# Second and fourth feed-forward of a fused FP32 transformer kernel: the norm's token factor moved from the input rows to the gate and up results

## The reference, cut to what matters

```python
def rms_norm(x, g):
    y = xf * lax.rsqrt(jnp.mean(xf * xf, axis=-1, keepdims=True) + EPS)
    return y * g
def modulate(h, shift, scale):
    return h * (1.0 + scale[:, None, :]) + shift[:, None, :]
def swiglu(h, w_in, w_out):
    g, u = jnp.split(h @ w_in, 2, axis=-1)          # 1024 -> 2 x 2816
    return (jax.nn.silu(g) * u) @ w_out             # 2816 -> 1024
h = modulate(rms_norm(x, norm_g), sh, sc)
x = x + 0.5 * (1.0 + gate)[:, None, :] * swiglu(h, w_in, w_out)
```

## Time and profile before

| | |
|---|---|
| median of 3 runs | 1314.43 us |
| profiled execution, whole | 1312.69 us |
| its span, first to last instruction | 1310.9 us |
| TensorE matmul busy | 1258.1 us (96%) |
| VectorE busy | 1068.6 us (82%) |
| ScalarE busy | 633.6 us (48%) |
| chain that ended last | PE 88%, DVE 7%, ACT 2% |
| granted TensorE clock, mean | 0.994 of full |

### The profile page before, as it was taken

One profiled execution on the slowest core, in us unless ns is written; L12 is line 12 of the kernel. 1 busy time (PEld: TensorE's weight loads), 2 busy tenths in 40 slices (PEclk: granted clock), 3 DMA queues, 4 the chain that ended last, 5 costly groups with the idle time before them and its releaser, 6 DMA issues.

```text
span 1310.9 us, 26643 instructions
## 1 busy us (share of the span) xinstructions
PE 1258.1 (96%) x10570; PEld 1227.8 (94%) x10570; DVE 1068.6 (82%) x1668; ACT 633.6 (48%) x994; POOL 187.2 (14%) x203
## 2 busy tenths in 40 slices
PE   1999999999999999999999999999999999999996
PEld 1999999899999889999999999999999989999996
DVE  6998988898787777988878778999977588895674
ACT  2534334443434556554346653343455675455453
POOL 5598800000000000000001000000000014530000
PEclk8999999999999999999999999999999999999999
DMA  9998887399888359988863379887655698555561
GB/s 356 394 329 314 295 316 270 131 319 336 304 311 286 129 193 358 331 303 306 309 207 112 113 245 331 302 304 262 217 179 184 114 186 179 169 163 178 175 194 50
DMA packets 110924, 319.73 MB, mean 244 GB/s; under 512 B 24096, under 2 KB 35808, under 8 KB 110560
## 3 DMA queue, kind: packets, MB, share of 16 engines
q1 hardware_dynamic: 110816, 318.23, 73.0%
HBM read 313.18 MB, written 5.01 MB: 243 GB/s over the span
## 4 chain that ended last, share of the span: by engine, by line
PE 88%; DVE 7%; ACT 2%; issue 1%; DMA 1%; SPq 1%; ACTq 0%; DVEq 0%
PE tiles L375 18%; PE tiles L377 18%; PE tiles L376 18%; PE acc L375 8%; PE acc L376 8%; PE acc L377 8%; PE nrm L551 1%; DVE w_lo L367 1%; PE tiles L577 1%; DVE arena L1474 1%; PE tiles L579 1%; PE tiles L594 1%; DMA arena<-in_gstream 1%; ACT w_hi L363 1%; DVE arena L1429 1%
## 5 line engine op out<-in xcount | busy, mean ns | idle before, releaser
L363 ACT CAST w_hi<-land 128x1024 fp32r<-128x1024 f32 x391 | 408.4, 1047 | 452.1 <-PE tiles L377 282.4
L367 DVE TENSOR_TENSOR w_lo<-land,w_hi 128x1024 fp32r<-128x1024 f32 x391 | 484.0, 1245 | 145.9 <-ACT w_hi L363 144.6
L375 PE MATMUL tiles<-x_hi,w_hi 128*128 128x256 f32 x1384 | 393.8, 285 | 0.8 <-DVE arena L1874 0.5
L376 PE MATMUL tiles<-x_lo,w_hi 128*128 128x256 f32 x1384 | 391.9, 283 | 0.0
L377 PE MATMUL tiles<-x_hi,w_lo 128*128 128x256 f32 x1384 | 391.8, 283 | 0.0
L375 PEld LDWEIGHTS tiles<-x_hi,w_hi 128*128 128x128 f32 x1384 | 265.7, 192 | 3.0 <-issue 1.0
L376 PEld LDWEIGHTS tiles<-x_lo,w_hi 128*128 128x128 f32 x1384 | 265.8, 192 | 0.1
L377 PEld LDWEIGHTS tiles<-x_hi,w_lo 128*128 128x128 f32 x1384 | 265.8, 192 | 0.0
L1429 DVE SCALAR_TENSOR_TENSOR arena<-arena 128x1024 f32<-128x1024 f32 x184 | 227.2, 1239 | 12.3 <-ACT arena L1157 9.5
L375 PE MATMUL acc<-h_hi,w_hi 128*128 128x256 f32 x704 | 199.4, 283 | 0.0
L376 PE MATMUL acc<-h_lo,w_hi 128*128 128x256 f32 x704 | 199.3, 283 | 0.0
(11 more groups left out here) (338 smaller groups left out, 1601.1 us busy)
## 6 DMA issues: line engine op xcount, KB each, us to landing
land<-in_stream SPq DMA_DIRECT2D x391, 512.0 KB, 4.5
arena<-in_gstream SPq DMA_DIRECT2D x184, 512.0 KB, 6.4
w_dram<-arena SPq DMA_DIRECT2D x3, 512.0 KB, 6.4
arena<-w_dram SPq DMA_DIRECT2D x6, 256.0 KB, 9.2
arena<-in_c_rows SPq DMA_DIRECT2D x2, 512.0 KB, 5.7
x<-in_x_t SPq DMA_DIRECT2D x1, 1024.0 KB, 9.5
arena<-in_ssm_bn SPq DMA_DIRECT2D x1, 1024.0 KB, 8.6
u_dram<-arena SPq DMA_DIRECT2D x1, 1024.0 KB, 5.3
```

The source lines that it names most:

```text
L363: nc.scalar.copy(w_hi[:, u % RING], land[:, u % LAND]).then_inc(hi_done, 1)
L367: nc.vector.tensor_tensor(w_lo[:, u % RING], land[:, u % LAND], w_hi[:, u % RING].bitcast(F32), ALU.subtract).then_inc(lo_done, 1)
L375: nc.tensor.matmul(outs, lh, rh, start=first, stop=False, **kw)
L376: nc.tensor.matmul(outs, lh, rl, start=False, stop=False, **kw)
```

## The change

Only FFN 1 and FFN 3 (`LATE`) are changed. Their input rows no longer hold the token factor or the shift: ScalarE makes x_hi as x times the feature factor (`late_rows` of ScalarE), VectorE x_lo of the same. To each k row of 256 tokens two more columns are added that hold the shift (`late_shift`), so every gate and up matmul has 258 columns, and column 256 of a result is what the shift contributes to it. Gate and up get a PSUM bank each (`quad`, four banks). For each tile, ScalarE copies the two shift results out (`late_shifts`), VectorE multiplies gate and up by the token factor (`late_scale`, 128 x 512), ScalarE does silu with the shift as bias (`late_silu`), VectorE adds the up shift and multiplies (`late_hidden`), ScalarE makes the high part (`late_hi`), VectorE the low part (`late_lo`). One weight split stands between each two of these on both engines. TensorE's order becomes g0 u0 g1 u1 g2 o0 u2 g3 o1 u3 and so on to g21 o19 u21 o20 o21; the weights are stored in that order.

The squares' sum is taken inside `first_units`, between the products with the high and those with the low input, over four tiles that VectorE has added in pairs. The filler products ahead of both feed-forwards go. On VectorE the coefficients of FFN 1, its shift columns and one weight split move ahead of the pooling updates; at the end of both feed-forwards one weight split moves from before the updates of x to behind them.

```diff
-            sum_squares(2)
-            keep_busy(7)
-            ffn(1, 2)
+            ffn_late(1, 2)
...
+            def pair_sums(e):
+                for k in range(0, KT, 2):
+                    pe.wait_ge(sq_pair, 4 * e + k // 2 + 1)
+                    m = nc.tensor.matmul(late_sum, ones, t_buf[:, k], start=(k == 0), stop=(k == KT - 2))
+                m.then_inc(nrm_done, 1)
+            def ffn_late(f, stage):
+                wait_bank(pe, o0)
+                wait_bank(pe, o0 + 1)
+                pe.wait_ge(shift_cols, 2 * (e + 1))
+                first_units(base, [quad[:, b, 0:T + 2] for b in range(3)], xs_hi, xs_lo, KT * stage,
+                            between=lambda: pair_sums(e))
+                late_unit(3, base + 3, 0)
...
+                            pe.wait_ge(silu_done, i * 4 + (FFN_TILES * f + j - 1))
+                            late_unit(2 * (j % 2), g_unit(f, j), i)
+                            out_unit(f, j - 2, o_unit(f, j - 2), i, 4)
+                            pe.wait_ge(freed["d"], i * 4 + (nd + j - 1))
+                            late_unit(2 * (j % 2) + 1, u_unit(f, j), i)
...  ScalarE
+            def late_rows(stage, n, ready, unit, before=None):
+                nc.scalar.activation(eps_root, con("eps", 1), ACT.Sqrt)
+                for k in range(KT):
+                    ready(k)
+                    nc.scalar.activation(x_hi[:, k], x[:, k], ACT.Identity,
+                                         scale=coef[:, stage, k:k + 1]).then_inc(xh_done, 1)
+                for k in range(KT):
+                    nc.scalar.square(t_buf[:, k], x[:, k]).then_inc(sq_done, 1)
+                split_hi(act, unit)
+                split_hi(act, unit + 1)
+                act.wait_ge(nrm_done, n + 1)
+                nc.scalar.activation(rx_late, late_sum, ACT.Sqrt, bias=con("eps", 1), scale=1.0 / D)
+                nc.scalar.activation(eps_root, con("eps", 1), ACT.Silu)
...
+                            late_shifts(f, j - 2, i, 4)
+                            split_hi(act, o_unit(f, j - 2), i)
+                            late_silu(f, j - 2, i, 4)
+                            split_hi(act, u_unit(f, j), i)
+                            late_hi(f, j - 2, i, 4)
+                            split_hi(act, u_unit(f, j) + 1, i)
...  VectorE
+            norm_coef(2)
+            late_shift(2, 0)
+            split_lo(dve, UNIT["ffn1"] + 1)
             for k in range(KT):
                 wait_tile(dve, TILE["pool"] + k)
                 update(k, tiles[:, k % 2, 0:T], 1, freed["d"])
-            split_lo(dve, UNIT["ffn1"] + 1)
-            norm_coef(2)
             split_lo(dve, UNIT["ffn1"] + 2)
-            root(2)
-            norm_t(2)
+            late_rows(2, 2, 0, UNIT["ffn1"] + 3)
...
+            def late_rows(stage, n, e, unit):
+                (8 x) x_lo = x * factor - x_hi
+                (4 x) t_buf[k] = t_buf[k] + t_buf[k + 1]
+                split_lo(dve, unit)
+                split_lo(dve, unit + 1)
+                dve.wait_ge(rt_done, n + 1)
+                link(V.reciprocal(rx_late, rx_late))
...
+                            late_scale(f, j - 2, i, 4)
+                            (s = 0) split_lo(o(j-2)); late_hidden(f, j - 2, i, 4)
+                            (s = 1) split_lo(u(j)); late_lo(f, j - 2, i, 4)
+                            (s = 2) split_lo(g(j+1))
```

More of the change, by code:

```diff
@@ L589, in first_units @@
                         high(c, k)
+                if between is not None:
+                    between()
                 for c in range(3):
@@ new lines, in late_hi, with ffn_late @@
+            def late_hi(f, j, i, per):
+                nd = OWNER[:TILE[f"ffn{f}"]].count("d")
+                act.wait_ge(freed["d"], i * per + (nd + j + 1))
+                act.wait_ge(used, i * 3 * per + (FFN_BASE[f] + 3 * j))
+                nc.scalar.copy(h_hi[:, j % 2], gate_up[:, j % 2, 1]).then_inc(late_hh, 1)
+            def ffn_late(f):
+                base = FFN_BASE[f]
+                j0 = 2
+                for part, (reps, _) in enumerate(SEGMENTS[f]):
+                    with act.Fori(0, reps) as i:
+                        for m in range(4):
+                            j = j0 + m
+                            late_shifts(f, j - 2, i, 4)
[4 more added lines that the diff above has]
+                            split_hi(act, u_unit(f, j) + 1, i)
+                    j0 += 4 * reps
+                late_shifts(f, FFN_TILES - 2, 0, 0)
+                late_silu(f, FFN_TILES - 2, 0, 0)
+                late_hi(f, FFN_TILES - 2, 0, 0)
+                late_shifts(f, FFN_TILES - 1, 0, 0, 0, 1)
+                split_hi(act, base + 65)
+                late_silu(f, FFN_TILES - 1, 0, 0)
+                split_hi(act, base + 66)
+                late_shifts(f, FFN_TILES - 1, 0, 0, 1, 1)
+                late_hi(f, FFN_TILES - 1, 0, 0)
@@ L1436, in hidden @@
             def hidden(f, j, i, per):
-                base, nd = FFN_BASE[f], OWNER[:TILE[f"ffn{f}"]].count("d")
-                J = FFN_TILES * f + j
+                nd = OWNER[:TILE[f"ffn{f}"]].count("d")
+                J, plain = FFN_TILES * f + j, FFN_TILES * sum(n not in LATE for n in range(f)) + j
                 dve.wait_ge(silu_done, i * per + (J + 1))
@@ new lines, in late_rows @@
+            def late_rows(stage, n, e, unit):
+                for k in range(KT):
+                    dve.wait_ge(xh_done, KT * stage + k + 1)
+                    V.scalar_tensor_tensor(out=x_lo[:, k], in0=x[:, k], scalar=coef[:, stage, k:k + 1],
+                                           in1=x_hi[:, k].bitcast(F32), op0=ALU.mult,
+                                           op1=ALU.subtract).then_inc(xl_done, 1)
+                for k in range(0, KT, 2):
+                    dve.wait_ge(sq_done, KT * n + k + 2)
+                    V.tensor_tensor(t_buf[:, k], t_buf[:, k], t_buf[:, k + 1], ALU.add).then_inc(sq_pair, 1)
+                split_lo(dve, unit)
+                split_lo(dve, unit + 1)
+                dve.wait_ge(rt_done, n + 1)
+                link(V.reciprocal(rx_late, rx_late))
@@ L1539, in ffn @@
             def ffn(f, stage, pre, gate_col, ahead_units, next_stage):
-                base, b = FFN_BASE[f], G_FFN[f]
-                for s in range(pre, 5):
-                    split_lo(dve, base + s)
-                hidden(f, 0, 0, 0)
+                base, b, late = FFN_BASE[f], G_FFN[f], f in LATE
+                if not late:
+                    for s in range(pre, 5):
+                        split_lo(dve, base + s)
+                    hidden(f, 0, 0, 0)
                 b += G_FIRST[f]
@@ L1566, in ffn @@
                                     out_part(5 * (part - 1) + OUT_AT.index(3 * m + s))
-                            hidden(f, j - 1, i, 4)
+                            if not late:
+                                hidden(f, j - 1, i, 4)
                             if f == 2:
@@ L1574, in ffn @@
                 blocks[0] = b
-                split_lo(dve, o_unit(base, 21))
+                if late:
+                    j = FFN_TILES - 2
+                    late_scale(f, j, 0, 0)
+                    gate_coef(stage, gate_col, 0.5)
+                    late_hidden(f, j, 0, 0)
+                    late_lo(f, j, 0, 0)
+                    late_gate(f, j + 1)
+                split_lo(dve, o_unit(f, 21))
                 if f == 0:
@@ L1579, in ffn @@
                         g_part(G_POOL, q, "silu")
-                hidden(f, 21, 0, 0)
-                for u in ahead_units[:2]:
+                if late:
+                    late_up(f, 21)
+                    late_hidden(f, 21, 0, 0)
+                    late_lo(f, 21, 0, 0)
+                else:
+                    hidden(f, 21, 0, 0)
+                for u in ahead_units[:1 if late else 2]:
                     split_lo(dve, u)
-                gate_coef(stage, gate_col, 0.5)
+                if not late:
+                    gate_coef(stage, gate_col, 0.5)
                 for k in range(KT):
@@ L1590, in ffn @@
                 norm_coef(next_stage)
-                split_lo(dve, ahead_units[2])
+                for u in ahead_units[1 if late else 2:]:
+                    split_lo(dve, u)
             dve.wait_ge(csilu_done, 1)
```

173 lines of the change are left out of this document (121 added, 52 removed).

## The result

The changed kernel takes 1300.76 us (1298.72 to 1303.90, four runs) against 1314.16 for the kernel before: ratio 0.9903 [0.9891, 0.9914], 13.4 us less. The forecast was 1310.2 and its range ended at 1306.5: the sign was right, the gain was three times the forecast. The changed kernel's runs lie 5 us apart, those of before 0.7.

The account below looks back on a forecast made before the run. TensorE, at work 96% of the span, was taken as the bound, VectorE nearly so. FFN 3 +4.9, FFN 1 +1.05, columns -1.8: net gain 4.2 us, 1314.43 to 1310.2, range 1306.5 to 1315.5.

Parts of the forecast that it names:

- the two columns: Gate and up matmuls of FFN 1 and 3: 2112 at 0.83 ns more each, 1.8 us lost; bounds 0 and 6.7 ns.
- the 13 ns: Every matmul: fixed cost on top of 0.417 ns a column, taken as independent of the width.
- The starts: Wanted work begins sooner without sum and filler ahead: FFN 3 gains 7.2 us, FFN 1 gains 4.95 us.
- The pair sums: Squares' sum now in TensorE's path inside the first units: eight passes cost 1.8 us in each late feed-forward.
- Waits at the start: TensorE waits for VectorE: ahead of g2 0.6 us (FFN 1) and 0.5 (FFN 3); FFN 1's o0 0.8, o1 0.7.
- The table load: On ScalarE's way to the first shifts: 1.28 us by the row; the skill's 2.66 would add about 0.9 us.
- The prediction's own sign: Gate and up matmuls: prediction is wrong if a 258-column matmul's pitch is not 0.121 us.
- The body: Steady rounds of both feed-forwards: no stall, 0 us, upper end 3; VectorE busy 0.2 to 0.4 us more a round.
- FFN 1 gives nothing or loses: Rival: FFN 1's 1.05 us margin vanishes, -1.5 there with doubled stalls and late pair sum, whole about 1313; 18%.

Follow-up runs that it names:

- e9: The changed kernel, unaltered, timed again beside the others of its set on one chip: 1301.46 us, ratio 0.9910.
- e11: The changed kernel with gate and up products of 256 instead of 258 columns, shift's contribution left out: 1298.27 us, ratio 0.9884.
- e3: The changed kernel with FFN 1 in its old form, only FFN 3 late: 1301.01 us, ratio 0.9901.
- e4: The changed kernel with FFN 3 in its old form, only FFN 1 late: 1304.30 us, ratio 0.9927.
- e13: The kernel before with 16 unused bytes ahead of x_hi: 1294.67 us, ratio 0.9855.
- e14: The kernel before with 64 unused bytes ahead of x_hi: 1298.44 us, ratio 0.9879.
- e5: The kernel before with 144 unused bytes ahead of x_hi: 1303.55 us, ratio 0.9928.
- e15: The kernel before with 400 unused bytes ahead of x_hi: 1303.44 us, ratio 0.9924.
- e16: The changed kernel with only FFN 3 late, rows of 258 values and 16 unused bytes ahead of x_hi: 1289.46 us, ratio 0.9812.
- e10: The kernel before at the changed kernel's exact addresses (rows of 258 values, 16 unused bytes behind them), second timing: 1303.87 us, ratio 0.9925.
- e2: The kernel before with an unused tensor of 144 bytes behind x_lo, shifting every later tensor: 1305.36 us, ratio 0.9933.
- e6: The kernel before with 144 unused bytes ahead of the landing slots, so all tensors move together: 1315.27 us, ratio 1.0012.

## Why the prediction was wrong, and where it was right

**The missing step** stands in the prediction's part on the two columns: "No row has 258 columns or rows of operands 1032 bytes apart. The bounds are 0 (if the 13 ns swallow them) and 6.7 ns". The new spacing was seen and only a loss was allowed for; no reason excluded a gain. And it was bounded for the 2112 wide matmuls, while the bytes also moved the operands of some 7000 others: the stages that the change does not touch were put at nothing without a reason. The 13 ns a matmul on top of the columns were taken as a constant of the engine, because 256 and 512 columns gave the same. In this kernel they change with the addresses, and to a lesser part with the pattern that TensorE is in: 13.3 ns with all rows at multiples of 1024 bytes from the rings, 10 to 13 in most other kernels here, 6.6 in the best stretch (113.3 less 256 x 0.417 = 106.7). That step is worth 9.6 to 10.5 us against a miss of 9.4; the change itself brought less than forecast, which hid a part of it.

A hint lay in the trace of before: all but some 40 of the more than 6000 distances in the feed-forwards are 120 ns within 1, while some 110 of the 256-column matmuls in the stages with waits follow at 116 to 118. I had read the pitch from two sums and not from single starts.

**The starts** were right. FFN 3: +7.2 forecast, 7.15 measured (82.78 to 75.63), with x_hi 0.35 us behind the projection. FFN 1: +4.95 forecast, 4.99 measured.

**The pair sums**: 1.8 each forecast. Eight passes last 1.54 us from start to start (254.55 to 256.09), and the matmuls on either side of the switch lose 0.19 more: 1.7.

**Waits at the start.** Ahead of g2 I had 0.6 and 0.5; from start to start TensorE loses 0.98 - 0.12 = 0.86, and 0.1 more on the next matmul, both times. The chain is the one that was walked (VectorE, then ScalarE):

```profile
258.57 1.23 DVE L389 TENSOR_TENSOR w_lo<-land,w_hi 128x1024 fp32r<-128x1024 f32 x1 [3.17 <-ACT w_hi L385]
259.71 1.75 DVE L1621 RECIPROCAL rh<-rh 128x256 f32<-128x256 f32 x1
261.58 0.69 DVE L1573 TENSOR_TENSOR arena<-quad,rh 128x512 f32<-128x512 f32 x1
```

```profile
258.44 0.47 ACT L1146 ACTIVATE rh<-acc,cons 128x256 f32<-128x256 f32 x1
258.93 1.28 ACT L1147 ACT_TABLE_LOAD   x1
260.22 0.20 ACT L1147 ACTIVATE eps_root<-cons 128x1 f32<-128x1 f32 x1
...
262.36 0.51 ACT L1159 ACTIVATE arena<-arena,shift_s 128x256 f32<-128x256 f32 x1 [0.94 <-DVE arena L1573]
```

The inverse ends at 261.46, scaling starts at 261.58, silu ends near 262.9. A pause also costs TensorE some 0.2 us beyond the wait itself (idle 0.70 in the row, 0.98 from start to start), which the walk had left out. Ahead of o0 I had 0.8 and of o1 0.7; they are 0.62 and 0.65 in the second execution (e9), 0.65 and 0.61 in the first.

The table load lasts 1.28 us and its successor starts 0.01 later, so the 2.66 us that the Trainium skill ("ScalarE: Activation LUTs", section "What ACT_TABLE_LOAD costs") gives for a switch do not show here either; ScalarE is not last in that chain.

**The columns**: 0.9 us a feed-forward forecast, 1.0 and 1.1 measured. Per wide matmul 1.0 ns for 0.83, so that step was nearly right too, at equal addresses. The pitch of a gate or up product with 258 columns is 119.6 ns in e9, for 118.6 with 256 columns in e11. The prediction's own sign, wrong if that pitch is not 0.121 us, had thus come up: it had 120.8. In the changed kernel's first profile FFN 3 was at 119.7 ns and took 192.3 us, in the second at 118.8 and 191.1: the same program, so part of the spread is in the pitch.

**The body**: no wait in either feed-forward, as forecast. VectorE's extra at equal addresses is 101.11 - 97.86 = 3.3 us in the 120 of FFN 1 (14 rounds) and 98.02 - 94.78 = 3.2 in the 100 of FFN 3 (11.7 rounds), 0.23 and 0.28 a round; forecast 0.2 to 0.4.

**The sum at equal addresses.** FFN 1: 4.99 - 5.51 = -0.5; forecast 1.05 less 0.9 for its columns, +0.15. Of the 5.51, 1.7 are pair sums, 0.97 g2, 0.62 and 0.65 the next two, 1.0 columns; 0.5 I could not place. FFN 3: 7.15 - 3.97 = 3.2, forecast 4.9 - 0.9 = 4.0. Together 2.7 for 4.15; the medians say 2.4, and e3 and e4 that it is all FFN 3's. The rival "FFN 1 gives nothing or loses" was thus the true one on the late form, at -0.5 us and not the -1.5 of its price, and had 18%. Without the addresses' gain the whole would have come out near 1311.8 (an estimate, 1314.2 less 2.4), inside the range.

**What stays open.** Why distances between operands change the pitch, which patterns a distance allows, and which of them TensorE falls into at the start of a stage or behind a break. The profile shows the starts and nothing below them. That more than one pattern is possible at the same addresses, that a break can change it, and that it differs between executions, is shown; which addresses are best can at present only be tried.

## What to carry to other kernels

When a change moves or pads data, run the old program at the new addresses before crediting the change: here that control took some 10 of 12 to 13 us. Look at single start-to-start distances of a saturated TensorE, not at its busy share; a distance of exactly one value, all operands on the same power of two, is a sign that a few unused bytes ahead of the moving operand may be worth over 1%. Such a gain is fragile: judge it from many runs, and try several leads.

## What the runs showed of the hardware that I had not expected

- With every row of x, a and h at a multiple of 1024 bytes from the weight rings, a 256-column fp32r matmul starts every 120.0 ns, within 1 ns, in every feed-forward; with 16 to 400 unused bytes ahead of x_hi (e13, e14, e5, e15) every 116.7 to 118.7 on average, at best 113.3 (e16, FFN 2). The Trainium skill ("TensorE: Matmul & The Clock Gate", section "Wait — 56ns, not 53.3ns?") gives columns / 2.4 GHz plus about 2.5 ns for matmuls back to back, measured there at 128 and 512 columns; an estimate from it for 256 columns is 109.2 ns. No stretch here reached it.
- At the same addresses a stage can run at 118.7 ns a matmul and, behind four small products, at 117.4 (FFN 2 of e10); in e15 the same break takes it from 117.3 to 118.7.
- It goes the other way where x is the weight operand: kv's 512-column matmuls start every 226.7 ns with x on the multiples (before, e2, e6) and every 232 to 233.4 off them, 1.0 to 1.3 us for the stage. Two rows of the changed kernel, 18 matmuls apart, give (459.37 - 455.18)/18 = 0.2328 us, for 0.2267 in the earlier trace rows:

```profile
455.18 0.39 PE L397 MATMUL acc<-w_hi,xs_hi 128*128 128x512 f32 x1
...
459.37 0.40 PE L397 MATMUL acc<-w_hi,xs_hi 128*128 128x512 f32 x1
```

- Off the multiples a program can also repeat less well: the kernel before and e6 stay within 0.7 to 3.1 us in each set (without the two long executions), the others within 0.9 to 10.1 us.
